# Encoder layer: merge and routing in two passes (sample, then prompt), q, k, v products in three bf16 passes

## The chip, the cores and the metric

The kernel runs on one core of a Trainium2 chip. The metric is the device time of one execution in microseconds (us). Before the change it is 2573.8 us, the median of 3 runs (2572.68 to 2574.16).

TensorE (PE) multiplies, its weight loads stand as PEld, VectorE is DVE, ScalarE is ACT, GpSimd is POOL, and SyncE is SP, whose queue issues most DMAs.

## The reference, cut to what matters

```
mod = silu(c) @ w_ada + b_ada          # six parts: shift, scale, gate, twice
h   = rms_norm(x, norm1_g) * (1 + sc1) + sh1
qa, ka, va, qb, kb, vb, ga, gb = split(h @ w_in)      # 1536 columns of q, k, v, 2048 of gates
oa  = global_attention(rope(norm(qa)), rope(norm(ka)), va) @ w_branch_a
ob  = window_attention(qb, kb, vb, rel_bias, sink) @ w_branch_b
x   = x + gt1 * ((sigmoid(ga) * oa + sigmoid(gb) * ob) @ w_out)
h2  = rms_norm(x, norm2_g) * (1 + sc2) + sh2
aff = softmax(h2 @ w_router)           # 16 experts
g, idx = top_k(aff.T, cap)             # each expert takes 2 n / 16 of n tokens
x   = x + gt2 * scatter(expert(h2[idx]) * g)
y   = rms_norm(x, norm_f_g)
```

All of it is computed for two groups with the same weights: a prompt of 256 tokens (2 tiles of 128) and a sample of 1024 tokens (8 tiles), each routed as a set of its own: 32 prompt rows and 128 sample rows for each expert. The width is 1024, the experts' inner width 2048. All data are float32.

## The kernel before, in words

Every engine's program is written out by hand. `plan_steps` makes one list of steps, and each engine walks the list and does its own part of each step; engines meet at semaphores. So the list sets the order on every engine, and a wait holds up everything behind it on that engine. Tiles t = 0, 1 are the prompt and t = 2 to 9 the sample.

A product written as three bf16 passes (`split_product`, L1403 to L1405) takes both operands as high and low bf16 halves: w_hi x_hi + w_hi x_lo + w_lo x_hi. To split something means two instructions: a copy to bf16 (the high half), and a subtraction that gives the low half.

The stages in order of time:

- Start: PE multiplies the first four of twelve chunks of `w_ada` (AR, AC); ACT and DVE normalise tiles (XP), PE transposes them and DVE modulates them (X, L1054) to `hT`, float32, all ten tiles kept. SP loads `w_ada` chunks 0 to 3, then `w_in` in three chunks to `wqkv` (L515, L524), tables, and tiles of x.
- G (L1472): for each tile three products of 512 columns, float32, from `hT` and `wqkv`. Around G(t) stand X(t+2), Q(t-1) (transposes of q and k), N(t) (norm and rotation on DVE, L1126 to L1154) and XP(t+3). `tab` (L1103 to L1110), 49 small instructions on DVE, prepares the rotation tables.
- Attention: 40 items of global, then 40 of window attention. During the window part POOL splits `hT` to `hTs` (HS, L676, L679). At the last item A2 (modulation factors) and WS(0) (the first merge weights split, ACT L919, DVE L1216) stand ahead of the last RB (reciprocals: DVE L1206, POOL L656).
- M: for each of 8 blocks m of 128 columns, both gates and both branches, for tokens in chunks of 512, 512 and 256, in three bf16 passes; ACT takes sigmoids (L956), DVE and POOL form and split `mergedS`.
- WO: `w_out` split (ACT L929, DVE L1222), between chunks 1 and 2 of the last block.
- O: ten tiles, prompt first: 48 matmuls of 512 columns each; XO adds x and normalises (DVE L1252 to L1256, ACT L964, L966), X2 transposes and modulates, RT gives router logits (L1625), AT turns the affinities (L1631, L1274). GT spreads gate rows (L1563, ACT L934 to L940).
- K: top_k on DVE: rounds of MAX8, FIND_INDEX8 and MATCH_REPLACE8 (L1062 to L1064). Four rounds over 256 values for the prompt, 16 rounds over 1024 values for the sample, the latter behind the last tile. I turns the ranks; POOL gathers both groups' rows (L700); PE transposes them (L1645, L1648), DVE modulates (L1294), POOL splits (L713, L716).
- Experts: for each of 16 experts 12 chunks of 2 MB are loaded, split (ACT L803, DVE L1302, the first eight halves POOL L751) and multiplied in three bf16 passes. `AHEAD` = 8 halves of expert 0 are split before its first product. Then the final norm.

Of the kernel before, what the change touches and what calls it, by code (L numbers as in the profile page):

```python
# [18 lines left out]
U32 = mybir.dt.uint32  # L19
ALU = mybir.AluOpType  # L20
# [58 lines left out]

def attention_items():  # L80
# [15 lines left out]
def plan_steps(items):  # L96
# [17 lines left out]
    hs = 0  # L114
# [6 lines left out]
    for i in range(len(items) + 4):  # L121
# [43 lines left out]
        if i >= first_b + 11 and i % 2 and hs < NT:  # L165
            s.append(("HS", hs))
            hs += 1
        if i == len(items):
            s += [("A2",), ("WS", 0)]
    assert hs == NT  # L170
    assert t == len(items) and pv == len(items) and len(normed) == len(items) // NPAIR and s_ac == 12
    for m in range(KD):
# [3 lines left out]
        s.append(("M", m, 1))  # L176
        if m == KD - 1:
            s += [("WO", 0), ("WO", 1)]
        s.append(("M", m, 2))
    for t in range(NT + 3):  # L180
        if t < NT:
            s.append(("O", t))
        if t == 0:
            s += [("GT", n) for n in range(4)]
        if 0 <= t - 1 < NT:
            s.append(("X2", t - 1))
        if 0 <= t - 2 < NT:
            s.append(("RT", t - 2))
        if 0 <= t - 3 < NT:
            s.append(("AT", t - 3))  # L190
        if t == 6:
            s.append(("K", 0))
        if t < NT:
            s.append(("XO", t))
    s += [("GT", n) for n in range(4, 8)]
    s += [("K", 1), ("I",)]
# [3 lines left out]
def t_jobs(step, items):  # L200
# [8 lines left out]
    if k == "I":  # L209
        return [(step, n) for n in range(5)]  # L210
# [3 lines left out]
def encoder(nc, x_p, x_s, c_p, c_s, w_ada, b_ada, n1g, w_in, qg, kg, sink, w_ba, w_bb, w_out, n2g, w_router,  # L214
# [25 lines left out]
    with ExitStack() as ctx:  # L240
# [27 lines left out]
        hT = at(0, KD, TOK)  # L268
        qT = at(10240, 2, NPAIR, TOK)
# [6 lines left out]
        wqkv = [at(R3 + CH * c, KD, 512) for c in range(3)]  # L276
# [48 lines left out]
        hid32 = at(B + 12032, 4, SLOTS)  # L325
        gt2S = at(B + 12672, D)
# [43 lines left out]
        ada_in = [sem(f"ada_in{n}") for n in range(6)]  # L370
        win_in, wr_in = [sem(f"win_in{n}") for n in range(3)], sem("wr_in")
# [116 lines left out]

        def on_of(g):
# [1267 lines left out]
```

## Time and profile before

| what | us |
|---|---|
| median of 3 runs | 2573.8 (2572.68 to 2574.16) |
| the profiled execution | 2572.49 |
| its span | 2570.7 |
| PE busy | 2384.8 (93%) |
| DVE, ACT, POOL busy | 1605.4, 1162.8, 1123.0 |
| G stage, first to last product | 40.0 to 279 |
| attention | 279 to 645.9 |
| M stage | 645.9 to 957.6 |
| O stage and routing, up to the first expert's first product | 957.6 to 1199.0 |
| experts and final norm | 1199.0 to 2570.7 |

The page divides the span into 40 equal slices with each engine's busy share in tenths. A timeline row has start, duration, engine, line, operation and tiles, the number of instructions merged, and in brackets the idle time ahead and what ended it.

### The profile page before, as it was taken

The numbers are of one execution on the slowest core, as the hardware profiler recorded it, in microseconds if no ns is written. First come the engines' busy times: TensorE is split into PE (matmuls) and PEld (weight loads), VectorE is DVE, ScalarE is ACT, GpSimd is POOL, SyncE is SP. The second block draws the span as 40 slices with busy tenths as digits, with TensorE's granted clock in tenths as the row PEclk, the third lists the DMA queues.
The fourth block names the chain that finished last, engine by engine and source line by source line (L and its number), as shares of the span: only waits on it lengthen the run. The fifth ranks groups of instructions, "written<-read, shape, count | busy, mean of one in ns | idle before, by whom it ended". The sixth has DMA issues, their size and how long they took to land.

```text
span 2570.7 us, 53875 instructions
## 1 busy us (share of the span) xinstructions
PE 2384.8 (93%) x23508; PEld 1712.8 (67%) x23508; DVE 1605.4 (62%) x2014; ACT 1162.8 (45%) x1468; POOL 1123.0 (44%) x721
## 2 busy tenths in 40 slices
PE   8999899998999999934899999999999999999993
PEld 3444477655555555523788888888888888888871
DVE  1643466556111125575888878887888878887862
ACT  2111455567111112330656655665556655556552
POOL 0000111146232331042657667776677666676640
PEclk9999899999999999956999999999999999999997
DMA  8100300220221103252889998999899998999965
GB/s 315 33 17 1 115 1 1 99 99 2 82 50 50 25 34 115 99 207 76 300 317 330 324 318 321 326 336 320 312 331 318 343 315 317 331 330 326 315 234 188
DMA packets 230113, 512.23 MB, mean 199 GB/s; under 512 B 7819, under 2 KB 35580, under 8 KB 229756
## 3 DMA queue, kind: packets, MB, share of 16 engines
q1 hardware_dynamic: 219324, 477.36, 52.3%
q0 software_dynamic: 10560, 31.46, 4.4%
q8 instruction: 186, 3.05, 0.5%
q14 instruction: 43, 0.35, 0.0%
HBM read 480.49 MB, written 28.31 MB: 198 GB/s over the span
## 4 chain that ended last, share of the span: by engine, by line
PE 85%; DVE 6%; POOL 2%; SPq 2%; ACT 1%; DMA 1%; issue 1%; DVEq 0%; POOLq 0%; ACTq 0%
PE ps L1403 21%; PE ps L1404 20%; PE ps L1405 20%; PE ps L1472 7%; PE ps L1688 4%; PE ps L1533 3%; PE ps L1545 3%; PE ps L1514 2%; DVE arena L1054 1%; DVE ti_s L1063 1%; DVE top_s L1062 1%; DVE arena L1064 1%; POOL arena L679 1%; PE ps L1625 1%; POOL arena L676 1%
## 5 line engine op out<-in xcount | busy, mean ns | idle before, releaser
L1403 PE MATMUL ps<-arena 128*128 128x160 bf16 (+2 forms) x5344 | 1308.6, 264 | 21.8 <-DVE arena L1335 8.3
L1404 PE MATMUL ps<-arena 128*128 128x160 bf16 (+2 forms) x5344 | 1308.6, 264 | 0.0
L1405 PE MATMUL ps<-arena 128*128 128x160 bf16 (+2 forms) x5344 | 1308.4, 264 | 0.0
L1302 DVE TENSOR_TENSOR arena<-arena 128x2048 bf16<-128x2048 f32 x376 | 919.2, 2450 | 193.3 <-ACT arena L803 192.3
L803 ACT ACTIVATE arena<-arena 128x2048 bf16<-128x2048 f32 x384 | 726.7, 1904 | 239.0 <-PE ps L1405 176.9
L1403 PEld LDWEIGHTS ps<-arena 128*128 128x128 bf16 x5344 | 524.1, 98 | 154.6 <-issue 27.0
L1405 PEld LDWEIGHTS ps<-arena 128*128 128x128 bf16 x5344 | 524.3, 98 | 127.8 <-issue 1.9
L1404 PEld LDWEIGHTS ps<-arena 128*128 128x128 bf16 x5344 | 524.3, 98 | 118.9 <-issue 1.4
L727 POOL TENSOR_TENSOR arena<-arena 128x320 bf16<-128x320 f32 x128 | 283.8, 2217 | 10.0
L724 POOL TENSOR_TENSOR arena<-arena,ones 128x320 bf16<-128x320 f32 x128 | 179.4, 1401 | 179.3 <-DVE arena L1335 179.0
L991 ACT ACTIVATE arena<-ps 128x160 f32<-128x160 f32 x256 | 77.4, 303 | 351.4 <-PE ps L1405 351.4
L1472 PE MATMUL ps<-arena 128*128 128x512 f32 x480 | 208.1, 593 | 3.0 <-DMA arena<-w_in 1.7
L656 POOL TENSOR_TENSOR arena<-ones,rinv 128x512 f32<-128x512 f32 x20 | 20.9, 1043 | 393.9 <-DVE rinv L1206 337.0
L1240 DVE TENSOR_TENSOR arena<-arena,ps 128x512 f32<-128x512 f32 (+1 forms) x48 | 26.6, 595 | 246.5 <-ACT arena L956 246.5
L1472 PEld LDWEIGHTS ps<-arena 128*128 128x128 f32 x480 | 90.3, 190 | 113.8 <-issue 109.5
L956 ACT ACTIVATE arena<-ps 128x512 f32<-128x512 f32 (+1 forms) x48 | 22.6, 523 | 263.5 <-PE ps L1405 263.5
L686 POOL TENSOR_TENSOR arena<-arena 128x512 f32<-128x512 f32 (+1 forms) x24 | 26.1, 1088 | 217.9 <-DVE arena L1240 217.9
L713 POOL TENSOR_TENSOR arena<-arena,ones 128x480 bf16<-128x480 f32 (+1 forms) x48 | 101.4, 2113 | 45.4 <-DVE arena L1294 45.4
L911 ACT ACTIVATE arena<-ps 128x512 f32<-128x512 f32 (+2 forms) x160 | 74.5, 494 | 102.4 <-PE ps L1533 97.8
L1533 PEld LDWEIGHTS ps<-ident,arena 128*128 128x128 f32 x752 | 81.7, 143 | 55.0 <-issue 44.7
L1054 DVE TENSOR_SCALAR arena<-ps,A,modT 128x128 f32<-128x128 f32 x160 | 52.8, 402 | 97.9 <-PE ps L1458 97.9
L1335 DVE TENSOR_TENSOR arena<-arena,ps 128x160 f32<-128x160 f32 x256 | 79.2, 310 | 55.3 <-POOL arena L727 38.4
(197 smaller groups left out, 2377.8 us busy)
## 6 DMA issues: line engine op xcount, KB each, us to landing
arena<-w_e_gate SPq DMA_DIRECT2D x64, 2048.0 KB, 9.1
arena<-w_e_up SPq DMA_DIRECT2D x64, 2048.0 KB, 9.5
arena<-w_e_down SPq DMA_DIRECT2D x64, 2048.0 KB, 9.2
arena<-w_ada SPq DMA_DIRECT2D x12, 2048.0 KB, 8.6
arena<-x_sample SPq DMA_DIRECT2D x16, 512.0 KB, 3.5
arena<-w_in SPq DMA_DIRECT2D x16, 512.0 KB, 5.3
arena<-w_in SPq DMA_DIRECT2D x3, 2048.0 KB, 21.0
arena<-w_out SPq DMA_DIRECT2D x2, 2048.0 KB, 8.0
```

Source lines behind the costliest of these rows:

```text
L713: gp.tensor_tensor(xeT[par][:, 0, d0:d1], src, ones[:, 0:d1 - d0].unsqueeze(2).to_broadcast([P, d1 - d0, SLOTS]), ALU.mult).then_inc(high, 1)
L724: gp.tensor_tensor(hidT[par][:, 0, f:f + 2], src, ones[:, 0:2].unsqueeze(2).to_broadcast([P, 2, SLOTS]), ALU.mult).then_inc(high, 1)
L727: gp.tensor_tensor(hidT[par][:, 1, f:f + 2], src, hidT[par][:, 0, f:f + 2], ALU.subtract).then_inc(hid_done, 1)
L803: ac.activation(split_half(slot, a)[0], stage_half(kind, a), ACT.Copy).then_inc(hi_done, 1)
L1302: ve.tensor_tensor(lo, stage_half(kind, a), hi, ALU.subtract).then_inc(lo_done, 1)
L1335: ve.tensor_tensor(hid32[:, f % 4], sil[:, f % 2], ps[:, f % 3, SLOTS:2 * SLOTS], ALU.mult)\
L1403: pe.matmul(out, w_hi, x_hi, start=start, stop=False)
L1404: pe.matmul(out, w_hi, x_lo, start=False, stop=False)
L1405: return pe.matmul(out, w_lo, x_hi, start=False, stop=stop)
L1472: ins = pe.matmul(ps[:, n % 5], hT[:, kk, t * P:(t + 1) * P], wqkv[c][:, kk, :], start=(kk == 0), stop=(kk == KD - 1))
L1533: ins = pe.transpose(b[:, q * P:(q + 1) * P], probs(i, hh)[:, (a + q) * P:(a + q + 1) * P], ident[:])
L1688: ins = pe.matmul(ps[32 * g:32 * g + 32, 5, 0:256], x, wv[n][:, kf, 256 * g:256 * g + 256], start=q + kf == 0 and x is x_hi and n == 0, st ...
```

## The change

- SP waits for the products AR(0), AR(1), AR(2) before it loads the three `w_in` chunks, because `wqkv` now lies where `w_ada` chunks 0 to 2 lie.
- `hT` keeps two tiles. Behind each modulation stands HL(t): ACT copies to bf16, DVE subtracts; `hTs` serves both G and M. HS is gone.
- WQ: the three `w_in` chunks are split, six copies of 2048 columns on ACT and six subtractions on POOL. G(0) stays float32; G(1) to G(9) are three bf16 passes.
- WS(0) moves one item later, behind the last RB; A2 moves into M. WS is split in two parts of 2048 and 1024 columns.
- M covers the sample only (16 chunks of 512). Then O, XO, X2, RT, AT of the eight sample tiles. Then M2: the eight blocks again for the prompt's 256 columns, with the merge weights loaded and split a second time (POOL subtracts the part of 2048, DVE the part of 1024).
- The sample's top_k works on two halves of 512 values side by side on 64 partitions; its 16 rounds (KR) stand among the M2 steps. `merge_halves` (KM) joins them.
- Behind M2: the prompt's two O tiles (the second in quarters, OL), the sample's gather and transposes (XS), the first expert's weight splits (FH on ACT, FL on POOL) among them, then the prompt's top_k and gather.
- First expert weights: the first chunk is loaded once M2(4) is done, the second after the last sample tile's x.

The list of steps:

```diff
     s += [("XP", 0), ("XP", 1), ("AR", 0), ("AR", 1), ("AC", 0), ("AR", 2), ("AC", 1), ("AR", 3), ("AC", 2),
-          ("AC", 3), ("A1",), ("X", 0), ("XP", 2), ("X", 1), ("tab",)]
+          ("AC", 3), ("A1",), ("X", 0), ("XP", 2), ("X", 1), ("HL", 1), ("HL", 0), ("tab",)]
+    s += [("WQ", c) for c in range(3)]
     for t in range(NT):
         s.append(("G", t))
         if t + 2 < NT:
-            s.append(("X", t + 2))
+            s += [("X", t + 2), ("HL", t + 2)]
...
-        if i >= first_b + 11 and i % 2 and hs < NT:
-            s.append(("HS", hs))
-            hs += 1
-        if i == len(items):
-            s += [("A2",), ("WS", 0)]
-    assert hs == NT
+        if i == len(items) + 1:
+            s.append(("WS", 0))
     assert t == len(items) and pv == len(items) and len(normed) == len(items) // NPAIR and s_ac == 12
     for m in range(KD):
         s.append(("M", m, 0))
...
+    ns = NT - PT_TILES
+    for p in range(ns):
+        s.append(("O", p))
+        if p == 0:
+            s += [("GT", n) for n in range(2)]
...
+        if p in (1, 3):
+            s.append(("WS", KD + p // 2))
+    s.append(("WS", KD + 2))
+    tail = {(0, 1): [("X2", ns - 1), ("RT", ns - 2), ("AT", ns - 3)], (1, 0): [("RT", ns - 1), ("AT", ns - 2)],
+            (1, 1): [("AT", ns - 1)], (2, 0): [("GT", 2)], (2, 1): [("GT", 3)], (3, 0): [("GT", 4)], (3, 1): [("GT", 5)], (4, 0): [("GT", 6)], (4, 1): [("GT", 7)]}
...
+    for m in range(KD):
+        for b in range(2):
+            s.append(("M2", m, b))
+            s += tail.get((m, b), [])
+        if m + 3 < KD:
+            s.append(("WS", KD + m + 3))
+        for _ in range((0, 1, 2, 3, 3, 3, 2, 2)[m]):
+            s.append(("KR", r))
...
+    s += [("FH", 0), ("FH", 1), ("FL", 0), ("O", ns), ("KM",), ("IS",), ("FH", 2), ("FH", 3), ("FL", 1), ("FL", 2), ("XO", ns), ("FL", 3), ("OL", 0), ("OL", 1), ("X2", ns),
+          ("OL", 2), ("RT", ns), ("OL", 3), ("XS",), ("XO", ns + 1), ("AT", ns), ("FH", 4), ("FH", 5), ("X2", ns + 1),
+          ("RT", ns + 1), ("AT", ns + 1), ("FL", 4), ("FH", 6), ("FH", 7), ("FL", 5), ("K", 0), ("I",)]
```

SP's loads of `w_in` and of the first expert's weights; POOL's WQ; ACT's HL; DVE's HL and rounds:

```diff
+            sp.wait_ge(t_done, job_at[(("AR", 0), 0)] + 1)
             sp.dma_start(wqkv[0], win_v[:, :, 0:512]).then_inc(win_in[0], 16)
...
+            sp.wait_ge(m2_done, 10)
             load_chunk(-1, 0)
+            sp.wait_ge(x1_ready, NT - PT_TILES)
             load_chunk(-1, 1)
...
+                if k == "WQ":
+                    c = s[1]
+                    for a, z in ((0, CH // 2), (CH // 2, CH)):
+                        gp.wait_ge(wq_hi, 2 * c + z // (CH // 2))
+                        gp.tensor_tensor(wqs[c][:, 1, a:z], wqkv[c].rearrange("p k n -> p (k n)")[:, a:z], wqs[c][:, 0, a:z],
+                                         ALU.subtract).then_inc(wq_lo, 1)
...
+                if k == "HL":
+                    t = s[1]
+                    ac.wait_ge(h_ready, t + 1)
+                    if t == PT_TILES:
+                        ac.wait_ge(wq_lo, 4)
+                    ac.activation(tile_of(hTs, t)[:, 0:KD], hT[:, t % 2], ACT.Copy).then_inc(hl_hi, 1)
...
+                if k == "HL":
+                    t = s[1]
+                    ve.wait_ge(hl_hi, (2, 1)[t] if t < 2 else t + 1)
+                    x = tile_of(hTs, t)
+                    ve.tensor_tensor(x[:, KD:2 * KD], hT[:, t % 2], x[:, 0:KD], ALU.subtract).then_inc(hl_done, 1)
...
+            def top_round(b, r, a):
+                rows = (NE, 64)[b]
+                v = top[b][0:rows, r * 8:r * 8 + 8]
+                link(ve.max(v, a))
+                ve.max_index(ti[b][0:rows, r * 8:r * 8 + 8], v, a)
+                link(ve.match_replace(a, v, a, -1.0))
```

PE's G (waits and products), M2 (waits) and the prompt's last tile:

```diff
                         if t == 0:
                             pe.wait_ge(win_in[c], 16)
+                        elif c == 0:
+                            pe.wait_ge(hl_done, 1 if t == 1 else t + 1)
+                        if t == 1:
+                            pe.wait_ge(wq_lo, 2 * c + 2)
...
+                                x = tile_of(hTs, t)
+                                w = [wqs[c][:, q].rearrange("p (k n) -> p k n", k=KD)[:, kk] for q in range(2)]
+                                ins = split_product(ps[:, n % 5], [x[:, q * KD + kk] for q in range(2)], w,
+                                                    kk == 0, kk == KD - 1)
...
+                if k == "M2":
+                    m, b = s[1], s[2]
+                    n = 2 * KD + m
+                    if b == 0:
+                        pe.wait_ge(ws_done, 2 * KD + m + 1)
+                        pe.wait_ge(ws_rest, m + 1)
+                        if m < 2:
+                            pe.wait_ge(out_free, NT - PT_TILES - 1 + m)
+                        else:
+                            pe.wait_ge(mm_ready, n - 1)
...
+                if k == "OL":
+
+                    p, h, k0 = NT - 1, s[1] // 2, s[1] % 2 * 4
+                    if s[1] == 0:
+                        pe.wait_ge(mm_ready, 3 * KD)
+                        pe.wait_ge(merged_ready, 3 * KD)
+                        pe.wait_ge(out_free, p - 1)
+                    pe.wait_ge(wos_ready, 2 * h + 2)
+                    for kk in range(k0, k0 + 4):
+                        ins = split_product(ps[:, 2 * (p % 2) + h], [mergedS[0][:, n * KD + kk, P:2 * P] for n in range(2)],
+                                            [wos[h][:, n, kk * 512:(kk + 1) * 512] for n in range(2)],
+                                            kk == 0, kk == KD - 1)
+                    if s[1] == 3:
+                        ins.then_inc(out_done, 1)
```

## Rows read from the trace of the kernel before

**Rows 1.** The page's 40 slices: busy tenths of PE.
```profile
PE   8999899998999999934899999999999999999993
```

**Rows 2.** Windows: length, busy us (instructions) of each engine, TensorE clock, DMA share, GB/s.
```profile
645.90:957.60 311.70, 311.70 (x1730) 169.02 (x1728) 54.91 (x56) 45.08 (x56) 95.40 (x71) 1.00 0.17 47
957.60:1048.30 90.70, 88.16 (x478) 48.41 (x478) 47.47 (x106) 29.05 (x44) 10.91 (x16) 1.00 0.31 110
1048.30:1122.40 74.10, 59.57 (x310) 40.23 (x308) 41.05 (x128) 19.36 (x36) 4.21 (x8) 0.80 0.44 164
1122.40:1182.40 60.00, 2.05 (x12) 1.86 (x11) 58.91 (x82) 17.09 (x11) 32.28 (x8) 0.53 0.40 140
1182.40:1199.00 16.60, 4.53 (x22) 3.02 (x23) 5.38 (x23) 0.00 (x0) 7.90 (x12) 0.50 0.14 40
```

**Rows 3.** The chain that ended last, G stage: start, us, what.
```profile
86.60 0.45 PE ps L1458 x4
...
87.08 2.65 DVE arena L1054 x8
...
90.21 20.60 PE ps L1472 x48
```

**Rows 4.** Timeline of ACT, M stage: the sigmoids behind three chunks, widths 512, 256, 512.
```profile
910.85 1.08 ACT L956 ACTIVATE arena<-ps 128x512 f32<-128x512 f32 x2 [11.80 <-PE ps L1405]
918.71 0.66 ACT L956 ACTIVATE arena<-ps 128x256 f32<-128x256 f32 x2 [6.78 <-PE ps L1405]
934.25 1.08 ACT L956 ACTIVATE arena<-ps 128x512 f32<-128x512 f32 x2 [14.88 <-PE ps L1405]
```

**Rows 5.** Timeline of POOL: four subtractions of 2048 columns, beside the sample's top_k.
```profile
1126.97 16.14 POOL L751 TENSOR_TENSOR arena<-arena 128x2048 bf16<-128x2048 f32 x4 [20.32 <-ACT arena L803]
```

**Rows 6.** Timelines of ACT and DVE at the start: tile 2's norm, `tab`'s first and last.
```profile
60.57 1.06 ACT L842 ACTIVATE arena<-arena 128x1024 f32<-128x1024 f32 x1 [25.74 <-DMA arena<-x_sample]
...
65.60 0.21 DVE L1103 TENSOR_TENSOR arena<-arena,gains 128x64 f32<-128x64 f32 x1
...
71.15 0.69 DVE L1110 TENSOR_SCALAR arena<-arena 128x1024 f32<-128x1024 f32 x1
```

**Rows 7.** Timeline, first expert: a DVE and a POOL instruction, both between SBUF tiles.
```profile
1222.83 2.29 DVE L1302 TENSOR_TENSOR arena<-arena 128x2048 bf16<-128x2048 f32 x1 [0.80 <-ACT arena L803]
1222.90 2.87 POOL L727 TENSOR_TENSOR arena<-arena 128x320 bf16<-128x320 f32 x1
```

**Rows 8.** Timeline of DVE, G stage: the first of N(1) and the last of XP(3).
```profile
92.20 0.82 DVE L1126 TENSOR_TENSOR arena<-arena 128x640 f32<-128x640 f32 x1 [1.47 <-ACT arena L869]
...
99.86 0.75 DVE L1114 TENSOR_SCALAR arena<-arena,rs 128x1024 f32<-128x1024 f32 x1
```

**Rows 9.** Timeline of PE, start: the products of the last early `w_ada` chunks.
```profile
31.02 3.17 PE L1437 MATMUL ps<-arena,cS 128*32 128x512 f32 x16 [1.21 <-DMA arena<-w_ada]
```

**Rows 10.** Timelines of ACT, DVE and PE ahead of the M stage.
```profile
635.29 2.75 ACT L919 ACTIVATE arena<-arena 128x3072 bf16<-128x3072 f32 x1
...
638.15 3.36 DVE L1216 TENSOR_TENSOR arena<-arena 128x3072 bf16<-128x3072 f32 x1 [3.02 <-ACT arena L919]
...
642.86 2.07 PE L1554 MATMUL ps<-ident,arena 128*128 128x128 f32 x8 [6.59 <-POOL arena L656]
```

**Rows 11.** Timeline of PE, O stage: two GT; transposes of two tiles in turn.
```profile
972.63 2.02 PE L1563 MATMUL ps<-arena,ones 128*128 128x128 f32 x16 [0.17 <-DVE arena L1232]
...
996.08 1.04 PE L1458 MATMUL ps<-ident,arena 128*128 128x128 f32 x8
...
1009.02 1.04 PE L1458 MATMUL ps<-ident,arena 128*128 128x128 f32 x8
```

**Rows 12.** Timeline of DVE: the second round over 256 values, its MAX8.
```profile
1053.95 0.42 DVE L1062 MAX8 top_p<-yeP 16x8 f32<-16x256 f32 x1
```

**Rows 13.** Timeline of DVE: the last O tile's first instruction, the last affinity's copy.
```profile
1099.13 1.22 DVE L1252 TENSOR_TENSOR arena<-ps,arena 128x1024 f32<-128x1024 f32 x1
...
1116.41 0.28 DVE L1274 COPY arena<-ps 16x128 f32<-16x128 f32 x1 [0.29 <-PE ps L1631]
```

More of the change, by code:

```diff
@@ L208, in t_jobs @@
         return [(step, 0)]
-    if k == "I":
-        return [(step, n) for n in range(5)]
+    if k in ("IS", "I"):
+        return [(step, n) for n in range(2 if k == "IS" else 3)]
     return []
@@ L646, in _, with gather_rows, gather, low_first @@
                 gp.wait_ge(const, 6 + q)
+            def gather_rows(b):
+                gp.indirect_dma_start(out=(xeP, xeS)[b], out_offset=None, in_=xn_d[b],
+                                      in_offset=bass.IndirectOffsetOnAxis(ap=gidx[b][:, 0:1], axis=0)).then_inc(gat[b], 16)
+            def gather():
+                gather_rows(1)
+                gather_rows(0)
+            def low_first(h):
+                kind, slot = first_half(h)
+                hi, lo = split_half(slot, h % 2)
+                gp.wait_ge(hi_done, h + 1)
+                gp.tensor_tensor(lo, stage_half(kind, h % 2), hi, ALU.subtract).then_inc(lo_done, 1)
             for s in steps:
@@ L689, in _ @@
                     gp.wait_ge(mhigh, n + 1)
-                    gp.tensor_tensor(mergedS[:, KD + s[1], cols], tmp, mergedS[:, s[1], cols], ALU.subtract)\
+                    gp.tensor_tensor(dst[:, KD + s[1], a:a + w], tmp, dst[:, s[1], a:a + w], ALU.subtract)\
                         .then_inc(merged_ready, 1)
+                if k == "WS" and s[1] >= KD:
+                    m = s[1]
+                    gp.wait_ge(ws_hi, 2 * m + 1)
+                    raw_at, w_at = merge_weights(m)
+                    w = half_words(w_at, 2, MW)[:, :, 0:2 * KD * P]
+                    gp.tensor_tensor(w[:, 1], at(raw_at, 2 * KD * P), w[:, 0], ALU.subtract).then_inc(ws_rest, 1)
@@ L756, in _ @@
             gp.wait_ge(idx_ready, 5)
-            for b in range(2):
-                gp.tensor_copy(gidx[b][:], idx[b][:, 0:1]).then_inc(cidx, 1)
+            gp.tensor_copy(gidx[0][:], idx[0][:, 0:1]).then_inc(cidx, 1)
             gp.wait_ge(cidx, 2)
-            gather()
-            for n in range(3):
-                split_rows(0, n + 1, n, 0)
+            gather_rows(0)
+            low_first(6)
+            gp.wait_ge(xe_mod, 3)
+            dst = xeT[0][:, :, :, CAP_S:SLOTS]
+            gp.tensor_tensor(dst[:, 0], xp32, ones[:, 0:KD].unsqueeze(2).to_broadcast([P, KD, CAP_P]), ALU.mult)\
+                .then_inc(high, 2)
+            gp.wait_ge(high, 3)
+            gp.tensor_tensor(dst[:, 1], xp32, dst[:, 0], ALU.subtract).then_inc(xe_ready, 3)
+            low_first(7)
             gp.tensor_tensor(spare[:, 2:3], ones[:, 0:1], ones[:, 1:2], ALU.add).then_inc(ye_free, 1)
@@ L1567, in _ @@
                     m, c = s[1], s[2]
[L1568 to L1569 removed]
+                    n = 2 * m + c
                     if n == 0:
@@ L1665, in gate_up @@
                 for half in range(2):
-                    slot = ring(3 * q + half)[1]
+                    slot = first_slot(q, half) if e == 0 else ring(3 * q + half)[1]
                     wv = [half_words(split[slot] + n * CH // 2, KD, 512) for n in range(2)]
```

465 lines of the change are left out of this document (291 added, 174 removed).

## The prediction

> **What bounds the kernel now.** I read the page's slices first. PE is at 9 tenths nearly everywhere, with one hole, slices 17 to 20 [rows 1]. Behind the hole come the experts at a full PE; the change leaves them as they are, so whatever brings the first expert's first product forward brings the end forward as much. Next I cut the time between the attention and that product (1199.0) into windows [rows 2]. In the M stage PE works for all of its 311.7 us. The O stage costs 88.2 busy us of 90.7. Then 60.0 us in which DVE alone works, on the sample's ranks, and 16.6 us of turning ranks, gathering and splitting. From the attention's end to 1199.0 that makes 553.1 us. Last, the chain of waits in the G stage [rows 3]: per tile 20.60 us of products and 3.6 us between two tiles, 2.65 of them a modulation on DVE.
>
> **The change part by part.** Times are the profiled execution's (span 2570.7, whole 2572.5); the median 2573.8 lies 1.3 above it, and I subtract from the median.
>
> *G, per tile.* Two bf16 sigmoids stand 15.54 us apart over a chunk of 72 matmuls of 512 columns [rows 4], 0.2158 each. A G tile in three passes is 72 such, 15.54 against 20.60: 5.06 saved. The 3.6 us between tiles stay. Does DVE keep up with 19.1 us a tile? From the end of G(t): modulation done at 3.1, q transposes at 3.6, ACT's evacuation and high copy to some 6.4, DVE's subtraction and k copy to 8.2, then N and XP, which take 8.4 from first to last [rows 8]: 16.6. It fits with 2.5 to spare. G(2) to G(9) save 8 x 5.06 = 40.5.
>
> *G, the splitting of the weights.* ACT is held by XP(2) until tile 2's x lands at 60.57; the modulation of X(1) ends where `tab` began, 65.6 [rows 6]. Two HL copies bring ACT to 67.8, the first copy of 2048 (two thirds of the 2.75 for 3072 columns, so 1.8 [rows 10]) to 69.7. From there POOL needs six subtractions of 4.03 [rows 5], 24.2: to about 94. G(1)'s third product waits for the last. That alone puts its end at 99.1 and G(2) at 102.8 instead of 90.2.
> What decides more is `tab`. One POOL instruction of 128x320 that began 0.07 us behind a DVE one took 2.87 us: it ended 0.65 behind it, so it had stood still while DVE worked [rows 7]. Both have two inputs in SBUF, as `tab` (49 instructions in 6.2 us, [rows 6]) and POOL's subtractions have. If whoever holds the way keeps it for its whole instruction and they take turns, DVE gets one small instruction in behind each 4 us of POOL. Then POOL ends at 95, some ten of `tab`'s are done, the others end at 100, X(2) at 103, HL(2) at 105, N(0) and XP(3) at 113.6, X(3) 3.6 later, and G(2) starts at 117 to 118: 27 late. Without turns it is 12.6 late. I take the turns, the nearer row. 40.5 - 27 - 1.5 (PE's clock is at 0.50 after a long pause [rows 2], some 3 us at half speed) = **12 saved**; the other end is 26.
> The Trainium skill (SBUF — State Buffer, "Who interferes with whom") says the same for a `tensor_tensor` with both inputs in SBUF against a GpSimd instruction that reads SBUF: the second to come blocks fully. By that rule the 12 stands; a reader who knows only PE's and ACT's work would write 26. The trace's one pair of rows agrees, though no row shows f32 against POOL's long ones.
>
> *SP's new waits.* At 31 PE still waited for a `w_ada` chunk [rows 9]; AR(0), some 8 us and two chunks earlier, lets `w_in` queue behind it in time, and the tables behind that: nothing, 2 at most. *HS gone*: POOL was off PE's path in the window part except in its first groups: 0, at best 3.
>
> *M's start.* WS(0) stood ahead of the last reciprocals: DVE's 3.36 ended at 641.5 and PE stood 6.59 us before OT [rows 10]. Now reciprocals come first; ACT's first part (1.8) and DVE's (2.3) end at about 640.5: **5.3 saved**. If TE copies on ACT come in between, 3.
>
> *M, O, M2.* M is 16 chunks: 248.6. WO starts one chunk earlier than it is needed; both halves take 14 to 15 us under 15.54: nothing, 2.5 if late. O: seven tiles took 90.7, of which 2.5 idle (PE busy 88.16) [rows 2], and two of four GT move on, 2.0 [rows 11]; so 86.1. The eighth adds 12.9 (the period, [rows 11]), with X2, RT, AT behind it 2.7: 101.7. M2: a chunk of 256 columns is 7.86 [rows 4], eight are 62.9; the sample's last X2, two RT, ATs and six GT add 10.3: 73.2. The same columns cost the same; what the second staging costs is off PE: POOL 4.03 + 2.1 (merge) under 7.86 a block, ACT 2.75 + 0.7, DVE 1.2 + 0.8. DVE has the ranks too: a round cost 60/16 = 3.75 over 1024 values; over 256 its three instructions take 0.42 each, with gaps 1.35 [rows 2, 12]; so 2.15 over 512, and 16 take 34.4. With all else DVE has some 63 us of work in 73. Blocks with three rounds and a GT are over PE's pace by 0.5 to 1, and PE may run two blocks ahead: cost 0, upper bound 12.
>
> *From M2's end (E) to the first product.* O(8) to E+10.4, rank transposes to 11; XO(8) keeps X2(8) until about 18 while half of the last tile fills in; RT(8), the rest of O(9): E+26. From the last tile's first DVE instruction to its last affinity took 17.3 [rows 13]: E+43, with ACT's XS ahead of it in the queue already within the rows' slack. Prompt ranks 4 x 1.35 + 0.9: E+49.3. Ranks to first product took 16.6 [rows 2]; one gather less (1.3) and 256 columns split instead of 1280 (3): 12.3, E+61.6. POOL's first-expert subtractions take turns with XO and KM: 1.4. **63** in all; bounds 57 (no half clock) and 75. The weights: chunk 0 and 1 land before E; chunk c=7 may be asked for at E+67, and is first split some 20 us into the expert: nothing.
>
> Sum: 248.6 + 101.7 + 73.2 + 63 = 486.5 against 553.1: 66.6 saved. 2573.8 - 12 - 5.3 - 66.6 = **2490**.
>
> **The rivals.**
> 1. `tab` isn't held up (POOL's and DVE's turns don't cost DVE): G saves 26, so 2476. For: `tab` would have fewer columns than POOL in each turn and might slip in several. Against: [rows 7]. Chance 0.15.
> 2. M2 or the tail is bound by DVE, ACT and POOL: the ranks stand in line with the sigmoid products, and a block waits for a staging that waits for a block. M2 +8 to 12 and the tail at 75: 2505 to 2515. For: DVE's 63 of 73. Against: three staging buffers. Chance 0.25.
> 3. The G stage isn't PE's any more (the change doesn't do what it says): ACT evacuates behind Q, HL waits for ACT, N for HL, and the period stays at 24.2. The 40.5 are lost: 2530. Against: 16.6 of 19.1. Chance 0.07.
> 4. Slower: the clock. The pause before G(1), some 13 us, takes TensorE to its lower level, 1.2 GHz, and it does not come back while each tile has its 3.6 us gap. A tile costs 31.1 instead of 15.5, nine of them +140: 2630, slower than before. It decides from 84/15.5 = 5.4 such tiles on. Against: the same gaps stood before with the products at full speed [rows 3], and M runs at 1.00 [rows 2]. Chance 0.02.
>
> **How the numbers follow.** The forecast (2484 to 2496) has 0.51. Low end: rival 1 with the tail at 57 and HS at 3 gives 2467, and WO or O better by some us 2464. High end: forecast with M2's 12 and half of the tail's 12 more, 2508, some 4 of M's start and WO, 2512. Outside lie rivals 3, 4 and a third of 2. A measurement of this kernel tells 0.2% (5 us) from no change; all cases but rival 4 and something unseen (0.01) are faster by more: 0.97 faster, 0.01 within, 0.02 slower.
>
> **What would show it.** G(2)'s first product at 117 (not 103, not over 120); L1103's successors, short instructions, strung out one per POOL subtraction; later G tiles 19.1 apart. M starting 17 earlier. M2 with PE full, 73 long. No DVE-only stretch of 60; instead some 63 from the last M2 product to the first expert's, in which PE is about half busy. First product at 1115. It is wrong if the tiles stand over 20 apart, if M2 exceeds 80, or if the experts, brought forward 84 us, end by less: that would mean that their loads, not PE, set their pace.

## The result and the profile after

The changed kernel takes 2540.3 us, the median of 4 runs (2537.7 to 2541.5), beside 2574.0 for the kernel before: a ratio of 0.9868, with the 95% interval 0.9851 to 0.9885. It is faster by 34 us. The forecast was 2490 with a range of 2464 to 2512: the direction was right, and some 50 of the 84 us did not come. The profiled execution took 2540.2 us with a span of 2538.4, 32.3 less than before. Every whole time below is the median of four or five executions, except that one of e10's four took 6134.5 us, which no trace explains, and is left out of its median.

The page's slices of the kernel after, PE and its clock:

```profile
PE   8599899998999998587899999999999999999993
...
PEclk9799899999999999797999999999999999999997
```

The hole behind the merge is shallower and longer: slices 16 to 20 have 8, 5, 8, 7, 8 tenths, where slices 18 to 20 had 3, 4, 8 [rows 1]. Slice 2 has a new hole of 5, the pause ahead of G(1). Windows of the kernel after, cut at its stages: G, attention, M, O (eight sample tiles), M2 (from its first product to its last), and from there to the first expert's first product (it begins at 1165.4). Columns as in [rows 2]:

```profile
40.00:263.70 223.70, 184.84 (x834) 90.94 (x848) 134.34 (x352) 56.58 (x128) 24.84 (x6) 0.93 0.13 48
263.70:625.70 362.00, 341.39 (x3067) 231.76 (x3068) 214.85 (x299) 224.66 (x526) 62.65 (x58) 0.97 0.17 56
625.70:874.30 248.60, 247.79 (x1136) 112.70 (x1152) 67.32 (x53) 42.87 (x49) 77.58 (x47) 1.00 0.22 62
874.30:978.00 103.70, 101.44 (x550) 56.35 (x557) 61.02 (x122) 34.49 (x51) 19.56 (x19) 1.00 0.59 178
978.00:1103.60 125.60, 87.88 (x668) 75.08 (x668) 76.52 (x140) 36.31 (x51) 39.65 (x29) 0.84 0.33 97
1103.60:1165.60 62.00, 33.86 (x166) 19.95 (x168) 35.53 (x97) 27.42 (x32) 41.31 (x23) 0.74 0.50 180
```

Against the forecast, stage by stage:

| stage | forecast | measured |
|---|---|---|
| G ends earlier by | 12 | 15.2 |
| M starts earlier by | 17.3 | 20.2 |
| M | 248.6 | 248.6 |
| O | 101.7 | 103.7 |
| M2 | 73.2 | **125.6** |
| M2's end to the first expert's product | 63 | 61.8 |

The experts carried forward what they were given: their first product came 33.6 us earlier (1165.4 for 1199.0) and the span ended 32.3 earlier. So one term of the sum is wrong, M2, by 52 us. What PE waited for in M2 (us in total, times, longest):

```profile
PE ps L1748 <- DVE arena L1390: 34.0, 6, 10.4
PE ps L1859 <- ACT lg L1097: 3.5, 1, 3.5
```

L1748 is GT, the spreading of a gate's row over the partitions by a product of ones with `dg`; L1390 is DVE's making of `dg`. The six GT that the change moved into the blocks of M2 wait, every time: 7.6, 2.7, 8.0, 2.7, 10.4 and 2.7 us. One lap of what holds them up, in the timelines of ACT, DVE and POOL of the kernel after (start, us, line, what, idle time before it and what ended that):

```profile
1028.01 0.60 ACT L1049 ACTIVATE arena<-ps 128x512 f32<-128x512 f32 x1 [3.73 <-PE ps L1748]
1028.50 2.85 ACT L1032 ACTIVATE arena<-arena 128x2048 bf16<-128x2048 f32 x2
1033.27 0.38 ACT L1084 ACTIVATE arena<-ps 128x256 f32<-128x256 f32 x1 [1.92 <-PE ps L1580]
1043.30 0.76 ACT L1053 ACTIVATE arena<-ps 32x256 f32<-32x256 f32 x2 [9.64 <-PE ps L1748]
```

```profile
1024.65 1.72 DVE L1390 TENSOR_SCALAR arena<-ident,modT 128x128 f32<-128x128 f32 x4
1031.38 4.25 DVE L1373 TENSOR_TENSOR arena<-arena 128x1024 bf16<-128x1024 f32 x1 [5.01 <-ACT arena L1032]
1035.55 0.68 DVE L1188 MAX8 top_s<-arena 64x8 f32<-64x512 f32 x1
...
1039.86 0.42 DVE L1403 TENSOR_TENSOR arena<-arena,ps 128x256 f32<-128x256 f32 x1
1040.20 0.87 DVE L1390 TENSOR_SCALAR arena<-ident,modT 128x128 f32<-128x128 f32 x4
```

```profile
1030.48 4.07 POOL L769 TENSOR_TENSOR arena<-arena 128x2048 bf16<-128x2048 f32 x1 [3.45 <-ACT arena L1032]
```

It is to be read as a ring. ACT copies GT(3) out of PSUM at 1028.0, and only behind that come its two copies of the next weights (L1032). DVE's subtraction of their last 1024 columns (L1373) waits 5.0 us for them, and then takes 4.25 us for work of 1.2, because POOL's subtraction of 4.07 us (L769) began 0.9 us ahead of it: it ends 1.1 us behind POOL's. Behind it stand two rank rounds of 2.15 us, behind them the product of the chunk whose sigmoid ACT had ready at 1033.7, and only behind that the `dg` of GT(4). PE, done with that chunk at 1033.3, gets it at 1041.2, and ACT copies GT(4) at 1043.3. Then it starts again. PE's rows of GT(2) and GT(4):

```profile
1017.37 2.04 PE L1748 MATMUL ps<-arena,ones 128*128 128x128 f32 x8 [7.61 <-DVE arena L1390]
...
1041.21 2.05 PE L1748 MATMUL ps<-arena,ones 128*128 128x128 f32 x8 [7.98 <-DVE arena L1390]
```

One lap takes 23.8 us, for a block that is 7.9 us of products at full clock and two GT of 1 us each.

### The profile page after: what moved, and what is told of

It is laid out like the page before. It is cut to its first block, busy times and chain, and to the rows that moved or that the text cites. A ratio compares the mean times of both kernels' runs of the same rounds, so it can differ in the third digit from the quotient of the medians.

```text
span 2538.4 us, 54391 instructions
## 1 busy us (share of the span) xinstructions
PE 2341.3 (92%) x23617; PEld 1698.3 (67%) x23724; DVE 1673.3 (66%) x2040; ACT 1214.5 (48%) x1520; POOL 1145.7 (45%) x713
## 4 chain that ended last, share of the span: by engine, by line
PE 82%; DVE 10%; ACT 3%; DMA 2%; issue 2%; SPq 1%; POOL 0%; DVEq 0%; ACTq 0%; POOLq 0%
PE ps L1579 22%; PE ps L1580 21%; PE ps L1578 21%; PE ps L1920 4%; PE ps L1730 4%; PE ps L1718 4%; PE ps L1699 2%; DVE arena L1181 2%; DVE arena L1373 1%; DVE arena L1251 1%; PE ps L1709 1%; ACT arena L1032 1%; DMA arena<-w_ada 1%; PE ps L1612 1%; DMA arena<-w_e_up 1%
## 5 line engine op out<-in xcount | busy, mean ns | idle before, releaser
L1579 PE MATMUL ps<-arena 128*128 128x160 bf16 (+2 forms) x5556 | 1394.8, 269 | 28.1 <-POOL arena L751 13.6
L1580 PE MATMUL ps<-arena 128*128 128x160 bf16 (+2 forms) x5555 | 1393.9, 269 | 0.2
L1578 PE MATMUL ps<-arena 128*128 128x160 bf16 (+2 forms) x5462 | 1360.0, 267 | 17.4 <-DVE arena L1510 7.7
L1578 PEld LDWEIGHTS ps<-arena 128*128 128x128 bf16 x5560 | 547.5, 98 | 196.5 <-issue 41.9
L1580 PEld LDWEIGHTS ps<-arena 128*128 128x128 bf16 x5560 | 547.4, 98 | 155.6 <-issue 3.3
L1579 PEld LDWEIGHTS ps<-arena 128*128 128x128 bf16 x5560 | 547.4, 98 | 145.3 <-issue 3.0
L1397 DVE TENSOR_TENSOR arena<-arena,ps 128x512 f32<-128x512 f32 x32 | 20.6, 684 | 176.2 <-ACT arena L1079 176.2
L806 POOL TENSOR_TENSOR arena<-arena,ones 128x480 bf16<-128x480 f32 (+1 forms) x45 | 98.9, 2198 | 33.6 <-DVE arena L1466 33.6
L1079 ACT ACTIVATE arena<-ps 128x512 f32<-128x512 f32 x32 | 17.4, 595 | 201.4 <-PE ps L1580 201.4
L1718 PE MATMUL ps<-ident,arena 128*128 128x128 f32 x752 | 110.3, 285 | 3.1 <-ACT arena L1005 1.4
L1333 DVE TENSOR_REDUCE nm<-ps 128x1 f32<-128x1024 f32 (+1 forms) x80 | 81.3, 1059 | 39.9 <-PE ps L1699 32.1
L1730 PE MATMUL ps<-arena 128*64 128x128 f32 x1504 | 101.2, 280 | 6.0 <-ACT arena L1016 5.1
```

The lines of the kernel that those rows point to most:

```text
L806: gp.tensor_tensor(xeT[par][:, 0, d0:d1], src, ones[:, 0:d1 - d0].unsqueeze(2).to_broadcast([P, d1 - d0, SLOTS]), ALU.mult).then_inc(high, 1)
L1333: ve.tensor_reduce(nm[:, i % 4, hh:hh + 1], src, AX.X, ALU.max, negate=True).then_inc(nm_ready, 1)
L1578: pe.matmul(out, w_hi, x_hi, start=start, stop=False)
L1579: pe.matmul(out, w_hi, x_lo, start=False, stop=False)
L1580: return pe.matmul(out, w_lo, x_hi, start=False, stop=stop)
L1718: ins = pe.transpose(b[:, q * P:(q + 1) * P], probs(i, hh)[:, (a + q) * P:(a + q + 1) * P], ident[:])
```

## The experiments

The cuts of code are abridged. Theory A: the ring. PE's GT waits for a `dg` that is queued on DVE behind everything of the block before. Rival B: DVE simply has too much to do while M2 runs, above all the ranks, and the order does not matter. Rival C: the turns between DVE and POOL alone (a turn: an instruction of the one stands still while the other's runs). Besides, theory T for the G stage: the same turns hold up `tab`, and through it tile 2. All times stand beside 7 or 8 runs of the kernel before on the same chip. The experiments ran on four chips, where that kernel took 2573.6 to 2574.6; so the numbers of two experiments compare to about 1 us, and less well where the executions of one lie far apart. "M2" is the time from the start of M2's first product to that of its last sigmoid (125.6 in the kernel after), "tail" the time from there to the first expert's first silu (67.8).

**e1: dg one block early.** `dg` becomes a step of its own, DG, that only DVE does:

```
+        if m in (1, 2, 3):
+            s += [("DG", 2 * m), ("DG", 2 * m + 1)]
         if m + 3 < KD:
             s.append(("WS", KD + m + 3))
         for _ in ...: KR
```

> VectorE's part of GT(2) to GT(7) (the four products with the identity) is issued one block earlier: behind the last product of M2(m-1,1) and ahead of the weights' subtraction and the ranks, instead of behind the product of the chunk that PE has just ended. Nothing else changes. Theory A (a ring: PE's GT waits for the dg that stands behind the ranks, the subtraction that stands behind ACT's copy, and this behind the copy of the GT before): PE's 34.0 us of waiting for L1390 go to under 3, with them most of the 12.7 us of half clock in the M2 stage; the stage shrinks from 125.6 to 80 to 86 us and the whole to 2494 to 2500 us. Rival B (VectorE simply has too much to do while M2 runs, in whatever order): the waits only move to the M2 products (L1578) and the stage keeps over 110 us; whole 2525 to 2540.

2499.7 us, ratio 0.9709 (0.9693 to 0.9725), 40.5 below the kernel after. PE's waits and the window of M2:

```profile
PE ps L1750 <- DVE arena L1392: 2.7, 1, 2.7
```

```profile
978.67:1062.54 83.87, 77.44 (x669) 68.56 (x666) 73.55 (x135) 36.27 (x51) 39.66 (x28) 0.96 0.45 130
```

M2 fell from 125.6 to 83.9, the waits for `dg` from 34.0 to 2.7, and the clock rose from 0.84 to 0.96. DVE did the same work and was busy 73.6 of 83.9 us. The theory's numbers came in; by B the stage would have kept over 110 us.

**e2: ranks behind M2.** The list of rounds is (0, 0, 0, 0, 0, 0, 0, 16), GT as in the change.

> All 16 rank rounds stand behind M2 instead of between its blocks; GT stays as it is. Rival B (VectorE's load, the ranks above all, is the cause): M2 falls from 125.6 to about 80 us, the ranks cost 29 us more behind it (34.4 less the 5.5 that stand there already), so the whole is 10 to 17 us faster, 2523 to 2530. Theory A (the ring): each GT still waits for the sigmoid, the product and the dg of the chunk just ended, 2.5 to 3.5 us, and in every second one for the subtraction too; of the 34.0 us of waiting 20 to 25 stay, the stage is some 110 us and the whole 10 to 20 us slower, 2550 to 2560.

2565.3 us, ratio 0.9967 (0.9953 to 0.9981): 25 slower than the kernel after, where I had said 10 to 20.

```profile
PE ps L1748 <- DVE arena L1390: 23.7, 6, 5.4
```

```profile
977.00:1090.50 113.50, 86.15 (x670) 73.89 (x669) 48.92 (x73) 36.25 (x50) 39.60 (x29) 0.88 0.37 107
1090.50:1194.80 104.30, 43.38 (x219) 27.24 (x218) 68.89 (x163) 27.56 (x33) 45.91 (x28) 0.66 0.30 108
```

With DVE at 48.9 busy us of 113.5, two thirds of the waits stay (23.7 of 34.0 us): they come from the order, and the ranks account for a third at most. M2 gained 12, the tail lost 36.5. The miss is in the tail. XO(8) began 27.3 us later after M2's end than in the kernel after, as counted; but then its addition fell into a turn. DVE, then POOL, of e2:

```profile
1129.77 9.93 DVE L1418 TENSOR_TENSOR arena<-arena 128x1024 f32<-128x1024 f32 x1
```

```profile
1129.46 1.04 POOL L712 DMA_INDIRECT arena<-xn_sample,gidx_s  x1 [0.58 <-POOL gidx_s L784]
1130.51 8.10 POOL L723 TENSOR_TENSOR arena<-arena 128x2048 bf16<-128x2048 f32 x2
```

1.2 us of work took 9.9: it began while POOL issued the gather, 0.7 us ahead of the subtractions, and ended 1.1 behind the second of two subtractions that POOL did without a gap. Why it lost is open: in the kernel after the same addition started just as far into the gather's issue (1115.61 behind 1115.31) and took 1.22. That is the 8.7 that I hadn't counted.

**e3: last columns first.** In the second staging ACT copies the last 1024 columns ahead of the first 2048, so that DVE's subtraction comes ahead of POOL's, which now waits for both copies. The copies' loop (the waits of DVE and POOL are changed to match):

```
-                    for a, z in ((0, 2 * KD * P), (2 * KD * P, MW)):
+                    for a, z in ((0, 2 * KD * P), (2 * KD * P, MW))[::1 if m < KD else -1]:
```

> In the second staging ACT copies the last 1024 columns of a block first and the first 2048 behind them, so that VectorE's subtraction (L1373) comes ahead of GpSimd's of 4.07 us and not within it. Same work. The L1373 rows in M2 fall from 4.2 to 5.0 us to 1.2, and end some 4.9 us earlier in each block. Theory A: the long ones of the six GT waits shrink by that, the other half stays: 10 to 22 us faster, 2518 to 2530, waits for L1390 at 15 to 24. Rival C (the engines' turns are the whole cause): waits for L1390 under 5 and the whole under 2505. Rival B (VectorE's load): the same as A here, about 20 faster, since 21 us of its 76.5 busy us go.

2520.7 us, ratio 0.98 (0.9783 to 0.9816): 19.6 below the kernel after. The waits of PE, then the groups by line of L1373 in M2, of the kernel after and of e3 (busy, mean ns of one | idle before):

```profile
PE ps L1748 <- DVE arena L1390: 22.9, 6, 5.7
```

```profile
L1373 DVE TENSOR_TENSOR arena<-arena 128x1024 bf16<-128x1024 f32 x6 | 26.7, 4458 | 20.8 <-ACT arena L1032 20.8
```

```profile
L1373 DVE TENSOR_TENSOR arena<-arena 128x1024 bf16<-128x1024 f32 x6 | 7.5, 1248 | 9.6 <-ACT arena L1032 9.5
```

4458 ns against 1248 for the same instruction: 3.2 us of turn in each of six. The turns are a part of the ring and not the whole (C falls). A and B had the same number here, so that this run alone would not tell them apart; e1 and e2 do.

**e4: the G part alone.** POOL's six subtractions of the weights go to DVE, `tab` behind XP(3):

```
+        if t == 0:
+            s += [("XP", 3), ("tab",)]
...
-                if k == "WQ":          # on POOL
+                if k == "WQ":          # on DVE, the same six instructions
```

> The G part alone: the six subtractions of the weights' low parts are done by VectorE (six of about 2.3 us) instead of GpSimd (4.14 each), behind HL(0); the table's 49 short instructions follow behind XP(3), ahead of N(0), with no GpSimd beside them. Theory T (turns: each short instruction that stood between two of GpSimd's waited 4 us for it, and this held N(0), XP(3) and with it G(2)): subtractions end at 82 instead of 93, the tables take 6.3 us instead of 29.7, G(2) starts at 102 to 104 instead of 115.2, the whole is 11 to 13 us faster, 2527 to 2529. Rival (VectorE's own work in that stretch is the limit, and 14 us more of it takes back what the turns cost): G(2) at 112 or later, 0 to 3 us faster.

2530.9 us, ratio 0.983 (0.9813 to 0.9846): 9.4 below the kernel after, a little less than the 11 to 13 expected. Timelines, first of the kernel after, then of e4:

```profile
68.09 24.84 POOL L751 TENSOR_TENSOR arena<-arena 128x2048 bf16<-128x2048 f32 x6 [65.02 <-ACT arena L967]
...
72.56 8.11 DVE L1251 TENSOR_TENSOR arena<-arena,gains 128x32 f32<-128x32 f32 x2
...
110.64 1.97 PE L1633 MATMUL ps<-ident,arena 128*128 128x128 f32 x8 [12.31 <-DVE arena L1260]
...
114.97 0.63 PE L1578 MATMUL ps<-arena 128*128 128x512 bf16 x1
```

```profile
68.54 13.30 DVE L1243 TENSOR_TENSOR arena<-arena 128x2048 bf16<-128x2048 f32 x6 [0.39 <-ACT arena L963]
...
101.43 1.11 PE L1669 MATMUL ps<-ident,arena 128*128 128x128 f32 x4 [9.58 <-DVE arena L1311]
...
104.46 0.63 PE L1581 MATMUL ps<-arena 128*128 128x512 bf16 x1
```

Two instructions that take 0.29 us together once POOL is done took 8.11: each stood still for one subtraction of POOL's. Without turns G(2) starts 10.5 us earlier, although DVE has 13.3 us more to do. T holds. The edit also moves `tab` behind XP(3), and that was not run by itself. In both kernels `tab`, N(0) and XP(3) all stand ahead of G(2), so the move should gain little; how much is not shown.

**e5: e1 and e3 together.**

> dg one block early (as in e1) and the last 1024 columns copied first in the second staging (as in e3). Theory A: in e1's M2 stage (84.5 us) PE still waited 3.5 us for RT, 2.7 for the first dg, both behind an L1373 of 4.2 to 5.0 us, and some 3 us went at half clock beside them. These go: stage 75 to 78 us, whole 2490 to 2494, 6 to 9 below e1. Rival: with dg early VectorE has slack enough, so that the turns cost nothing any more: 2497 to 2500, as e1.

2493.0 us, ratio 0.9685 (0.9668 to 0.9701). M2 took 79.3 us, the O stage 2.3 less. M2's window and its group of L1375 (the subtraction, as the line is numbered here):

```profile
976.26:1055.60 79.34, 75.86 (x669) 66.92 (x666) 67.92 (x135) 36.26 (x51) 39.65 (x28) 0.98 0.48 138
```

```profile
L1375 DVE TENSOR_TENSOR arena<-arena 128x1024 bf16<-128x1024 f32 x6 | 7.3, 1217 | 0.1
```

The 6.7 below e1 are within the expected 6 to 9; M2 itself came out 1 to 4 longer than I said, since the 2.7 of waiting for a `dg` stayed. It is GT(6)'s, the fifth of the six in M2, and not the first's, as I had read e1.

**e6: e5 and e4 together.**

> e5 and e4 together (dg early, last columns first, the weights' low parts on VectorE and the tables behind XP(3)). The G part is far from M2, so that the gains should add: 9.4 below e5, 2481 to 2485. Rival: what comes earlier in G is lost again at a later wait (weights for M or the experts not loaded yet): within 3 us of e5.

2482.4 us, ratio 0.9648 (0.9632 to 0.9664): 10.6 below e5, where 9.4 were expected. The gains add. Its four executions lie far apart, 2476.5 to 2485.3, and the profiled one is the fastest.

**e7: e1 with the ranks behind M2.** It prices what the ranks' cover is worth once the ring is cut.

> e1 with all 16 rank rounds behind M2. It prices the cover: if the rounds were free in e1's M2 stage, this one keeps 82 to 84.5 us, and the 29 us behind it come on top: 2525 to 2529. Rival B in its weaker form (VectorE's load still costs PE in e1, 74 busy us of 84.5): the stage falls to 75 or less and the whole is 2517 to 2521.

2529.4 us, ratio 0.9822 (0.9805 to 0.9838), 29.7 above e1 and 0.4 above the range. M2 took 79.6 us with DVE busy for 50.6, where e1's 83.9 had 73.6. That lies between the two guesses (82 to 84.5, and 75 or less): the rounds beside M2 cost PE some 4 us.

So some 30 us are saved by doing the ranks beside M2, once the ring is cut.

**e8, e9, e10: two further orders, without gain.** e8 moves the rounds one block earlier and runs O(9) in one with XO(9) ahead of X2(8), XS and RT(8); e9 and e10 each take one of the two.

```
-(0, 1, 2, 3, 3, 3, 2, 2)    +(0, 2, 3, 3, 3, 3, 2, 0)                        # e8, e9
-("OL", 0), ("OL", 1), ("X2", ns), ("OL", 2), ("RT", ns), ("OL", 3), ("XS",), ("XO", ns + 1)
+("OL", 0), ("OL", 1), ("OL", 2), ("OL", 3), ("XO", ns + 1), ("X2", ns), ("XS",), ("RT", ns)   # e8, e10
```

> e6, and two orders changed: the rounds stand one block earlier (none behind M2's last block), and of the prompt's two tiles O(9) is not split up any more: its four parts run in one, and XO(9) stands ahead of X2(8), XS and RT(8) on all engines. Theory (the tail hangs on XO(9), which started 0.6 us behind PE's last part of O(9), 29 us behind the last M2 product, of which PE stood or did other work for 6): XO(9) and the first expert's first product come 4 to 6 us earlier, 2476 to 2480. Rival (GpSimd's splits or the gather set the tail): within 2 us of e6.

> e6 with the rank rounds one block earlier (0, 2, 3, 3, 3, 3, 2, 0 behind the eight blocks, in place of 0, 1, 2, 3, 3, 3, 2, 2); the tail's order is e6's. It separates the two edits of e8. Theory: while the blocks still have GT and a subtraction, VectorE has about 10 us of work in a block of 9.8, and a third round there comes back as PE waits for dg: M2 stage 6 us longer, of which under 1 returns behind it; 2486 to 2489. Rival (e8's loss came from the tail's order): within 2 us of e6, 2480 to 2484.

> e6 with e8's order in the tail alone (O(9) in one, XO(9) ahead of X2(8), XS and RT(8)), the rounds where e6 has them. Theory (in e8's trace XO(9) came 5 us earlier after the last M2 product and RT(9)'s exponential not at all, 45.7 against 45.6): 2480 to 2484, as e6. Rival (the order gains and only the rounds' shift hid it): 2476 to 2479.

e8 2487.4 us (ratio 0.9667, 0.9651 to 0.9684), e9 2487.7 (0.9663, 0.9647 to 0.9679), e10 2482.8 (2481.7 to 2488.5; ratio 0.9647), against e6's 2482.4. e8 missed its 2476 to 2480; e9 and e10 came out inside their theories' ranges, 2486 to 2489 and 2480 to 2484. PE's waits in e9's M2, then in e10's tail:

```profile
PE ps L1753 <- DVE arena L1395: 7.1, 2, 4.9
```

```profile
PE ps L1864 <- DVE arena L1179: 12.2, 2, 10.4
```

In e9 the `dg` is late again: M2 85.2 for 79.3; the tail gives back 3.2 (65.9 for 69.1), more than I had allowed. In e10 the first instruction of XO(9) starts 6.4 us earlier after M2 (22.8 for 29.2), but its addition falls into a turn, 5.6 us for 1.2, and its square starts only 3.2 us earlier. The prompt's routing then stands behind X2(8), whose modulation had to wait for all of XO(9): the tail is 70.1. What came first only changed which of the two tiles waits.

**e11: Q ahead of X in the G stage, a miss.**

```
         s.append(("G", t))
+        if t >= 1:
+            s.append(("Q", t - 1))
         if t + 2 < NT: X, HL
```

> e6, and in the G stage Q(t-1) stands ahead of X(t+2) and HL(t+2) on all engines. In e6 PE stands 0.59 and 0.62 us in each of eight gaps, because two of Q's transposes wait for the banks that the modulation of X(t+2) frees on VectorE. With Q first the banks are freed by short copies: 0.6 to 1.2 us per tile, eight tiles: 5 to 9 us faster than e6, 2473 to 2478. Rival (the modulation ends later by as much, and HL, N and XP with it, so that the period stays 19.1): within 2 us of e6.

2493.2 us, ratio 0.9686 (0.967 to 0.9702): 10.8 slower than e6. PE, then ACT, of e11:

```profile
105.61 1.94 PE L1638 MATMUL ps<-ident,arena 128*128 128x128 f32 x8 [2.50 <-ACT arena L982]
```

```profile
103.14 0.60 ACT L952 ACTIVATE arena<-ps 128x512 f32<-128x512 f32 x1 [7.48 <-PE ps L1679]
...
104.79 1.16 ACT L982 ACTIVATE arena<-ps 128x512 f32<-128x512 f32 x2
```

I took the copies that free Q's banks for short, and they are; but on ACT they stand behind the tile's evacuation, 1.65 us of it. A wait of 2 x 0.6 for DVE became one of 2.5 for ACT, seven times, which makes some 9 of the 10.8.

**e12: the two dg of a block apart.** In e6 the 24 `dg` instructions of M2 took 20.0 us, 903 ns each. DG(2m) goes behind the first product of block m, DG(2m+1) behind the second.

```
             s.append(("M2", m, b))
             s += tail.get((m, b), [])
+            if m in (1, 2, 3):
+                s.append(("DG", 2 * m + b))
```

> e6 with the two dg of a block apart: one behind each of its products, instead of both behind the second. In e5 and e6 the pair, eight instructions of 0.2 us, takes 6.75 us three times, because GpSimd's subtraction of 4.07 us begins within it. Theory (turns between dg and GpSimd, VectorE being busy without a pause from the first GT on): the dg and the subtraction stand ahead of GpSimd's turn, VectorE gets back 4 to 5 us in each of three blocks, the last rank rounds end up to 8 us earlier after the last M2 product, of which O(8) on PE lets 3 through: the M2 stage stays at 76 to 78 us, the time from the last M2 sigmoid to the first silu falls from 69.1 to 66, whole 2477 to 2481. Rival (GpSimd's turn only falls on something else, the subtraction or a product): VectorE as busy as before, 2481 to 2484, or PE waits for dg again.

2476.5 us (2474.9 to 2477.4), ratio 0.9619 (0.9603 to 0.9635): the lowest median of all, 64 below the changed kernel and 98 below the kernel before. It is 5.9 below e6, but the two touch: e12's slowest execution took 2477.4, e6's fastest 2476.5. Groups of L1395, of e6 and of e12, and e12's M2 and tail:

```profile
L1395 DVE TENSOR_SCALAR arena<-ident,modT 128x128 f32<-128x128 f32 x24 | 20.0, 903 | 0.1
```

```profile
L1395 DVE TENSOR_SCALAR arena<-ident,modT 128x128 f32<-128x128 f32 x24 | 8.9, 432 | 0.3
```

```profile
968.10:1043.40 75.30, 73.67 (x669) 66.31 (x669) 61.67 (x143) 36.28 (x51) 41.65 (x29) 1.00 0.55 162
1043.40:1109.10 65.70, 37.86 (x216) 25.02 (x218) 36.12 (x93) 27.56 (x33) 46.61 (x28) 0.74 0.49 171
```

PE is busy in M2 for 73.7 of 75.3 us at a clock of 1.00 and no GT waits. M2 is 4.0 us shorter than e6's 79.3, a little below the 76 to 78 expected, and the tail is 3.4 shorter.

## Why the prediction was right and where it was wrong

**What failed: M2's 73.2, "PE may run two blocks ahead: cost 0, upper bound 12".** M2 took 125.6 us, far over the 80 that the prediction itself named as a sign of being wrong. The count of PE's own work was right: in e12 the stage has 73.7 us of it. Three things were missing.

1. *PE can't run ahead.* I placed the six GT as work of 1 us each on PE and did not ask what each waits for. `dg` stands on DVE behind the product of the very chunk that PE has just ended; so every GT drains PE, even with no rank in the way (e2: 23.7 us). The prediction compared DVE's work per block with PE's and took the surplus of 0.5 to 1 us for all that DVE could cost; it did not follow the order on DVE's queue.
2. *The subtraction's 1.2 us.* I had the turns in hand, [rows 7], and used them for `tab` alone. The same pair stands in each block of M2 and took 4.46 instead of 1.25 us, six times (e3).
3. *The clock.* With pauses of up to 10.4 us the granted clock over M2 was 0.84 and not 1.00: a mean of stretches at the lower level, 1.2 GHz, and at the upper, 2.4. PE was busy 87.9 us there for what takes 75.9 in e5.

The sum closes: from the kernel after to e5 the waits of PE in M2 fall from 37.7 to 3.4 (34.3) and its busy time from 87.9 to 75.9 (12.0), together 46.3; M2's lengths differ by 125.6 - 79.3 = 46.3. e12 takes off another 4.0, which leaves 2.1 of the 52.4 by which M2 missed the forecast.

**Rival 2 named the right kind** ("a block waits for a staging that waits for a block") with 8 to 12 us for M2, a quarter of the 52 measured at most, and had the tail at 75, where 61.8 was measured. DVE's total was not far off, "some 63 us": 61.7 busy us in e12, where few turns are left, 76.5 in the kernel after.

**G: 12, measured 15.2.** The mechanism was right in detail: POOL ended at 92.9 (95), `tab` at 97.2 (100), G(2) began at 115.0 (117 to 118), and L1251's rows are strung out as foretold, one instruction for each subtraction. I had forecast every step some 2 us later than it came. The term of 1.5 for the clock was too large as well: at G(2)'s start two products stand 0.43 us apart and not 0.22, which is 0.4 us. These two make up the 3.2. Later tiles stand 19.15 us apart (19.1), by ACT's evacuations at 134.74 and 153.89.

Rival 1 (no turns, 26 saved) was wrong for the change; e4, which takes them away, gets 10.5 of the 14 us by which the prediction's two cases of G(2) differ. The Trainium skill (SBUF — State Buffer, "Who interferes with whom") says that the engine which comes second to the shared port is blocked for the whole instruction of the first. The trace agrees for the L1251 rows and for L1373. It does not for e2's addition, by the start times of the rows: it started 0.7 us ahead of POOL's two subtractions and ended behind both. By the same page a `tensor_scalar` in a two-port mode takes part too. The 24 `dg` instructions are held up, 903 ns each in e6 and 432 in e12; that they run in such a mode no row shows.

**HS and M's start: 0 and 5.3.** M began 5.0 earlier behind the attention. The wait ahead of M's products is 2.5 us for the subtraction, [rows 10] had 6.6 for the reciprocals:

```profile
PE ps L1579 <- DVE arena L1373: 2.5, 1, 2.5
```

**M 248.6, O 101.7, tail 63.** M was exact. O had 103.7; 2.3 of it are turns of L1373 again, since with the last columns first it is 101.4. The tail had 61.8, with PE's waits as the prediction's steps put them, for XO, the prompt's ranks, the gather and POOL's split:

```profile
PE ps L1633 <- DVE arena L1420: 9.7, 2, 7.7
PE ps L1872 <- DVEq L1218: 6.6, 1, 6.6
PE ps L1888 <- DMA arena<-xn_prompt,gidx_p: 4.1, 1, 4.1
PE ps L1578 <- POOL arena L853: 3.5, 1, 3.5
```

**Rivals 3 and 4.** The G period is 19.15, not 24.2; and the clock came back after the pauses before G(1) and G(2) (1.00 from 120 to 250 in the kernel after), so that no later G tile took 31 us. But the clock did fall where PE paused again and again, in M2, where no case of mine had it.

**What stays open.** The two profiles of e6 and e12 end 0.9 us apart, e12's the later, although e12's M2 and tail are 7.4 us shorter. With the same code up to there e12 starts M 3.5 us later (616.6 for 613.1), its M is 1.6 longer, and what follows the tail 3.3 longer; I can't say why. So e12's gain is read from its two stages, and how much of it the whole keeps rests on the medians alone.

## What to carry to other kernels

When a step is moved between PE's products, follow its operand back on the other engine's queue to the last thing that depends on PE itself: if that is the product just ended, PE drains at each such step, here even with the ranks out of the way, and the remedy is to issue the operand one block earlier. Once two engines are known to take turns, look for every pair of them in the new order, and let the short instruction come first. A free engine with pauses is also a slower one: of the 46 us that the ring and the turns cost M2, 34 came as waiting and 12 as clock.

## What the runs showed of the hardware

- A DVE `tensor_scalar` of 128x128 float32 between SBUF tiles, 0.22 us alone (four in 0.87), is held up by POOL's `tensor_tensor` like one with two inputs: 0.90 us in the mean of e6's 24. In the tail of the kernel after even DVE's 128x16 scaling took 1.20 us instead of 0.23, and a CAST of 64x128 2.12 us, where e2's, with POOL idle, took 0.22:

```profile
1109.48 2.12 DVE L1198 CAST tif_s<-ti_s 64x128 f32<-64x128 uint32 x1
...
1129.27 1.20 DVE L1430 TENSOR_SCALAR af<-lg,rst 128x16 f32<-128x16 f32 x1
```

- The rank round over 64x512 and the modulation that reads PSUM are not held up. FIND_INDEX8 kept its 0.68 us and MATCH_REPLACE8 its 0.67 (at 1108.12 and 1108.78, within POOL's subtraction of 1107.46 to 1111.53), the modulation its 2.64 (at 1122.06, beside 1116.36 to 1125.23), all in the kernel after; MAX8 kept its 0.69 in e3 (at 1024.78, within 1023.33 to 1027.39). Such work is what to put beside POOL.
- POOL's next instruction can follow at once and keep DVE waiting for both (e2's 9.93 us for two of 4.05). In e2 and in e10 (5.62 us for 1.2) DVE's instruction had started 0.7 and 0.5 us ahead of POOL's subtraction and still waited; both times POOL was issuing DMAs as it started. That alone doesn't decide it, since the kernel after has the same order without the wait.
- Six pauses of PE of 2.7 to 10.4 us in the kernel after's M2 went with a granted clock of 0.84 over the 125.6 us; e12's M2, without them, had 1.00.
